# Key/value compression on TensorE: two tiles with strided rows, or four tiles with rows laid out by tap

## The reference, cut to what matters

```python
def compress(rows, pos_emb, w1, w2):
    B, T = rows.shape[0], rows.shape[1]
    r = rows.reshape(B, T // CMP_STRIDE, CMP_STRIDE, N_KV_HEADS, HEAD_DIM)   # CMP_STRIDE 16, HEAD_DIM 64
    w1h = w1.reshape(2, CMP_STRIDE, HEAD_DIM, HEAD_DIM)
    pe = pos_emb.reshape(2, CMP_STRIDE, 1, HEAD_DIM)
    lead = jnp.einsum('bnlgd,lde->bnge', r + pe[0], w1h[0])
    tail = jnp.einsum('bnlgd,lde->bnge', r + pe[1], w1h[1])
    return jnp.einsum('bnge,ef->bngf', jax.nn.silu(lead[:, :-1] + tail[:, 1:]), w2)
```

## Time and profile before

| | |
|---|---|
| timed runs | 1972.81, 1976.18, 1979.04 us |
| span of the profiled execution, first to last instruction | 1970.8 us |
| median of the timed runs less that span | 5.4 us |
| TensorE busy | 1854.6 us, 94% |
| VectorE, ScalarE, GpSimd busy | 888.9, 680.5, 173.2 us |
| mean DMA rate | 196 GB/s |

### The profile page before, as it was taken

The page is one execution under the profiler, slowest core; times in us unless marked ns, Lnnn a source line. Parts: engine busy times, 40 slices in busy tenths (PEclk is TensorE's granted clock), DMA queues, the critical chain, the costliest instruction groups (busy, mean ns, idle before and its releaser), DMA issues.

```text
span 1970.8 us, 34994 instructions
## 1 busy us (share of the span) xinstructions
PE 1854.6 (94%) x13870; PEld 1679.5 (85%) x13870; DVE 888.9 (45%) x1329; ACT 680.5 (35%) x813; POOL 173.2 (9%) x306
## 2 busy tenths in 40 slices
PE   4797589999999999999998999999999999999996
PEld 1297585885799999889996899999999999999995
DVE  1232132462644554545556544444444444444555
ACT  1122021562643443433334433333333333333333
POOL 1023000210322232101000100000000000000000
PEclk9689799999999999999999899999999999999998
DMA  9968864562844454487646544444455444443441
GB/s 363 407 240 242 213 232 173 210 263 104 318 162 161 160 162 151 169 303 308 242 171 241 198 159 169 170 155 140 160 169 194 164 170 156 163 170 132 162 164 58
DMA packets 67113, 386.81 MB, mean 196 GB/s; under 512 B 13661, under 2 KB 14077, under 8 KB 30062
## 3 DMA queue, kind: packets, MB, share of 16 engines
q1 hardware_dynamic: 50832, 346.39, 47.7%
q0 software_dynamic: 13904, 36.40, 6.9%
q10 hardware_dynamic: 2318, 3.19, 0.4%
HBM read 372.73 MB, written 13.20 MB: 196 GB/s over the span
## 4 chain that ended last, share of the span: by engine, by line
PE 82%; DMA 10%; DVE 3%; ACT 2%; ACTq 1%; issue 1%; SPq 0%; DVEq 0%
PE bank L635 24%; PE bank L637 23%; PE bank L636 23%; DMA raw<-in_w_units 10%; PE bank L738 3%; PE bank L646 3%; DVE wlo L345 1%; ACTq L973 1%; ACT whi L338 1%; PE bank L920 1%; PE bank L808 1%; PE bank L868 1%; PE bank L655 1%; PE bank L880 0%; PE bank L814 0%
## 5 line engine op out<-in xcount | busy, mean ns | idle before, releaser
L635 PE MATMUL bank<-xhi,wlo 128*128 128x288 f32 x2768 | 833.2, 301 | 38.2 <-DVE wlo L345 35.8
L636 PE MATMUL bank<-xlo,whi 128*128 128x288 f32 x2768 | 822.9, 297 | 0.0
L637 PE MATMUL bank<-xhi,whi 128*128 128x288 f32 x2768 | 819.7, 296 | 0.0
L345 DVE TENSOR_TENSOR wlo<-raw,whi 128x2048 fp32r<-128x2048 f32 (+1 forms) x251 | 532.8, 2123 | 544.1 <-ACT whi L338 536.5
L338 ACT CAST whi<-raw 128x2048 fp32r<-128x2048 f32 (+1 forms) x251 | 443.7, 1768 | 528.2 <-PE bank L637 390.2
L635 PEld LDWEIGHTS bank<-xhi,wlo 128*128 128x128 f32 x2768 | 525.1, 190 | 57.9 <-issue 42.0
L637 PEld LDWEIGHTS bank<-xhi,whi 128*128 128x128 f32 x2768 | 527.3, 191 | 0.0
L636 PEld LDWEIGHTS bank<-xlo,whi 128*128 128x128 f32 x2768 | 526.2, 190 | 0.4
L637 PE MATMUL bank<-hhi,whi 128*128 128x288 f32 x704 | 208.7, 296 | 0.0
L635 PE MATMUL bank<-hhi,wlo 128*128 128x288 f32 x704 | 208.0, 296 | 0.0
L636 PE MATMUL bank<-hlo,whi 128*128 128x288 f32 x704 | 205.2, 292 | 0.0
(11 more groups left out here) (275 smaller groups left out, 1460.9 us busy)
## 6 DMA issues: line engine op xcount, KB each, us to landing
raw<-in_w_units SPq DMA_DIRECT2D x284, 1024.0 KB, 5.4
raw<-in_w_ffn_out_units SPq DMA_DIRECT2D x64, 704.0 KB, 4.1
mgate<-mg POOLq DMA_DIRECT2D x32, 144.0 KB, 2.1
mgl<-mgate POOLq DMA_DIRECT2D x16, 288.0 KB, 5.3
toep<-rrow POOLq DMA_DIRECT2D x4, 1024.0 KB, 47.5
bz<-toep POOLq DMA_DIRECT2D x16, 192.0 KB, 2.7
xt<-in_x ACTq DMA_DIRECT2D x1, 2304.0 KB, 12.6
z<-in_x POOLq DMA_DIRECT2D x1, 2304.0 KB, 9.3
```

What stands on the lines that cost most here:

```text
L345: nc.vector.tensor_tensor(wlo[e][:, 0:size], raw[:, s, 0:size], f32(whi[e][:, 0:size]), ALU.subtract).then_inc(raw_used[s], 1)
L635: pe.matmul(acc, wlo[e][:, w], mh[:, c0 + kk, :], start=start and kk == 0, stop=False)
L636: pe.matmul(acc, whi[e][:, w], ml[:, c0 + kk, :], start=False, stop=False)
L637: m = pe.matmul(acc, whi[e][:, w], mh[:, c0 + kk, :], start=False, stop=stop and kk == kin - 1)
```

## The change

The cache pages and the embedding row come from the host laid out by tap: within each 128 positions, first tap 0 of the 8 chunks, then tap 1, and so on. GpSimd's copy of the prompt's rows makes the same order, in two copies. So one tap's columns are runs of 8 adjacent floats, one run per 128 positions. The lead and tail taps no longer accumulate in one place: for each of 16 taps there are four matmuls over all 16 chunks (19 x 16 = 304 columns), lead into the same half of bank 5, tail into the other half of bank 2, so that the four use the four quarters of the array. ScalarE copies the tail's halves from bank 2 to SBUF, swapping them back; VectorE adds lead (chunks 0 to 14) and tail (chunks 1 to 15) into `hsum`; ScalarE's Silu reads `hsum`, with the embedding row's sum as bias. TensorE waits in addition for bank 2 to be free. `wad` keeps only the two 64 x 64 blocks instead of a zero-padded 128 x 128, and GpSimd copies them in two steps. VectorE's last recurrent iteration is written out behind its loop to hold the second add.

```diff
-            one(pool.memset(cmp_rows[:, 2 * NSEQ, CMP:PAST], 0.0), rows_cp, 1)
+            one(pool.memset(cmp_rows[:, 2 * NSEQ, PAGE:PAST], 0.0), rows_cp, 1)
...
-                one(pool.tensor_copy(seqs[:, :, DEC_B, :], kvT[:, 0, 2 * kv:2 * kv + 2, 0:TP]), rows_cp, 2 + kv)
+                for g in range(2):
+                    one(pool.tensor_copy(seqs[:, g, DEC_B, :].rearrange("p (k l n) -> p k l n", k=2, l=STRIDE),
+                                         kvT[:, 0, 2 * kv + g, 0:TP].rearrange("p (k n l) -> p k l n", k=2, l=STRIDE)),
+                        rows_cp, 2 * kv + g + 2)
...
-                    one(pool.tensor_copy(wcur[:], wad[:, :, bass.ds(c, 1), :].squeeze(2)), wc_ok, c + 1)
+                    for h in range(2):
+                        half = slice(64 * h, 64 * h + 64)
+                        one(pool.tensor_copy(wcur[half, :, half], wad[half, :, bass.ds(c, 1), :].squeeze(2)),
+                            wc_ok, c * 2 + (h + 1))
...
-                pe.wait_ge(rows_cp, 2 + kv)
+                pe.wait_ge(rows_cp, 2 * kv + 3)
                 pe.wait_ge(gt_ok, 1)
                 after(pe, kc_ok, 2 * kv)
-                for l in range(CMP):
-                    for h in range(2):
-                        half = slice(64 * h, 64 * h + 64)
-                        ins = pe.matmul(bank[5][half, 0:(2 * NSEQ + 1) * NCMP], w1d[half, l, :],
-                                        cmp_rows[half, :, l:l + STRIDE * (NCMP - 1) + 1:STRIDE], start=l == 0, stop=l == CMP - 1)
+                pe.wait_ge(vt_ok, 1)
+                after(pe, rg_act, (RNN.n - 1) * 2 * kv)
+                rows = cmp_rows[:].rearrange("p r (k l n) -> p (r k) l n", k=2, l=STRIDE)
+                for l in range(STRIDE):
+                    for tap in range(2):
+                        for h in range(2):
+                            half = slice(64 * h, 64 * h + 64)
+                            to = half if tap == 0 else slice(64 - 64 * h, 128 - 64 * h)
+                            ins = pe.matmul(bank[5 if tap == 0 else 2][to, 0:CROWS * CHUNKS], w1d[half, l + STRIDE * tap, :],
+                                            rows[half, :, l, :], start=l == 0, stop=l == STRIDE - 1)
                 ins.then_inc(cmp_mm, 1)
...
                 act.wait_ge(cmp_mm, kv + 1)
+                after(act, cmp_sum, kv)
                 n = 2 * NSEQ * NCMP
-                nc.scalar.copy(cbias[:], bank[5][:, n:n + 1]).then_inc(cb_ok, 1)
-                act.wait_ge(cb_ok, kv + 1)
+                for h in range(2):
+                    nc.scalar.copy(tail[64 * h:64 * h + 64, :], bank[2][64 - 64 * h:128 - 64 * h, 0:CROWS * CHUNKS]).then_inc(tail_cp, 1)
+                act.wait_ge(cmp_sum, kv + 1)
                 dst = hk[:] if kv == 0 else hv[:].rearrange("p g s n -> p (g s n)")
-                nc.scalar.activation(dst, bank[5][:, 0:n], ACT.Silu, bias=cbias[:]).then_inc(cmp_act, 1)
+                nc.scalar.activation(dst, hsum[:, 0:n], ACT.Silu, bias=hsum[:, n:n + 1]).then_inc(cmp_act, 1)
...
+            def compress_sum(kv):
+
+                dve.wait_ge(tail_cp, 2 * kv + 2)
+                after(dve, cmp_act, kv)
+                lead = bank[5][:, 0:CROWS * CHUNKS].rearrange("p (r n) -> p r n", n=CHUNKS)
+                late = tail[:].rearrange("p (r n) -> p r n", n=CHUNKS)
+                v.tensor_tensor(hsum[:].rearrange("p (r n) -> p r n", n=NCMP), lead[:, :, 0:NCMP], late[:, :, 1:CHUNKS],
+                                ALU.add).then_inc(cmp_sum, 1)
...
                     split_lo(dve, RNN, i, j + 1)
+                    if kv is not None and j == 1:
+                        compress_sum(kv)
...
-            recurrent(0, False)
-            with dve.Fori(1, RNN.n) as i:
+            recurrent(0, False, 0)
+            with dve.Fori(1, RNN.n - 1) as i:
                 ch.loop(i - 1, 16)
                 recurrent(i)
-            ch.end(RNN.n - 1)
+            ch.end(RNN.n - 2)
+            recurrent(RNN.n - 1, True, 1)
             chain_rnn(2 * RNN.n - 1)
```

More of the change, by code:

```diff
@@ L38 @@
 NSEQ = 1 + DEC_B
+CROWS = 2 * NSEQ + 1
 H, KVH, HD = 16, 4, 64
@@ L42 @@
 STRIDE, CMP = 16, 32
-NCMP = PAST // STRIDE - 1
+CHUNKS = PAST // STRIDE
+NCMP = CHUNKS - 1
 DR = 1024
@@ L218, in build @@
         rrow = sbuf(p1, "rrow", [H, RV])
-        cmp_rows = sbuf(p1, "cmp_rows", [P, 2 * NSEQ + 1, PAST])
+        cmp_rows = sbuf(p1, "cmp_rows", [P, CROWS, PAST])
         rxp = sbuf(p1, "rxp", [P, LPAD])
@@ L227, in build @@
         hk = sbuf(p1, "hk", [P, 2 * NSEQ * NCMP])
+        tail = sbuf(p1, "tail", [P, CROWS * CHUNKS])
+        hsum = sbuf(p1, "hsum", [P, CROWS * NCMP])
         w1d = sbuf(p1, "w1d", [P, CMP, HD])
@@ L234, in build @@
         rb = sbuf(p1, "rb", [P, 2, RC])
-        wad = sbuf(p1, "wad", [P, 2, RC, P])
+        wad = sbuf(p1, "wad", [P, 2, RC, HD])
         convw = sbuf(p1, "convw", [P, 4, RC])
@@ L242, in build @@
         wcur = sbuf(p1, "wcur", [P, 2, P])
-        cbias = sbuf(p1, "cbias", [P, 1])
         p1.close()
@@ L309, in build @@
         rows_in, rows_cp, w1_in, cmp_mm, cmp_act = sem("rows_in"), sem("rows_cp"), [sem("w1k_in"), sem("w1v_in")], sem("cmp_mm"), sem("cmp_act")
+        tail_cp, cmp_sum = sem("tail_cp"), sem("cmp_sum")
         w2_mm, kc_ok = sem("w2_mm"), sem("kc_ok")
@@ L325, in build @@
         stored, y_out = sem("stored"), sem("y_out")
-        dve_c, pool_c, act_c, cb_ok = sem("dve_c"), sem("pool_c"), sem("act_c"), sem("cb_ok")
+        dve_c, pool_c, act_c = sem("dve_c"), sem("pool_c"), sem("act_c")
         def f32(ap):
@@ L437, in _ @@
             for n, (dst, v) in enumerate(((condp, 0.0), (f32(whi[0][:]), 0.0), (f32(wlo[0][:]), 0.0), (selt, 0.0), (rel1[32:33, :], 1.0),
-                           (w2b, 0.0), (wad, 0.0), (ones, 1.0 / D), (epst, EPS), (gs, 0.0))):
+                           (w2b, 0.0), (wcur, 0.0), (ones, 1.0 / D), (epst, EPS), (gs, 0.0))):
                 one(pool.memset(dst if isinstance(dst, bass.AP) else dst[:], v), pool_set, n + 1)
@@ L447, in _ @@
                 for w, name in enumerate(("lru_wa", "lru_wi")):
-                    pool.dma_start(wad[half, w, :, half],
+                    pool.dma_start(wad[half, w],
                                    a[name].rearrange("(c a) d e -> a d c e", a=2)[h]).then_inc(w_in_s, 16)
             one(pool.memset(rxp[:, 0:3], 0.0), st_pre, 1)
-            one(pool.memset(cmp_rows[:, 2 * NSEQ, CMP:PAST], 0.0), rows_cp, 1)
+            one(pool.memset(cmp_rows[:, 2 * NSEQ, PAGE:PAST], 0.0), rows_cp, 1)
             seqs = cmp_rows[:, 0:2 * NSEQ].rearrange("p (g s) t -> p g s t", s=NSEQ)
@@ L462, in load_rest @@
             def load_rest(kv):
-                pool.dma_start(cmp_rows[:, 2 * NSEQ, 0:CMP], a["cmp_pos"][kv]).then_inc(rows_in, 16)
+                pool.dma_start(cmp_rows[:, 2 * NSEQ, 0:PAGE], a["cmp_pos"][kv]).then_inc(rows_in, 16)
                 kv_written(pool)
-                one(pool.tensor_copy(seqs[:, :, DEC_B, :], kvT[:, 0, 2 * kv:2 * kv + 2, 0:TP]), rows_cp, 2 + kv)
+                for g in range(2):
+                    one(pool.tensor_copy(seqs[:, g, DEC_B, :].rearrange("p (k l n) -> p k l n", k=2, l=STRIDE),
+                                         kvT[:, 0, 2 * kv + g, 0:TP].rearrange("p (k n l) -> p k l n", k=2, l=STRIDE)),
+                        rows_cp, 2 * kv + g + 2)
             pool.wait_ge(b_in, SMALL)
@@ L763, in recurrent @@
                         pe.wait_ge(conv_ok, c + 1)
-                        pe.wait_ge(wc_ok, c + 1)
+                        pe.wait_ge(wc_ok, c * 2 + 2)
                         after(pe, rg_act, c)
@@ L1342, in chain_rnn, with recurrent @@
                                 gy[:, TP:T].rearrange("p (b s) -> p b s", s=DEC_S), ALU.mult).then_inc(y_ok, 1)
-            def recurrent(i, before=True):
+            def compress_sum(kv):
[5 more added lines that the diff above has]
+                                ALU.add).then_inc(cmp_sum, 1)
+            def recurrent(i, before=True, kv=None):
                 for j in range(4):
@@ L1649, in keys, with taps @@
         return np.ascontiguousarray(k_.reshape(n, t, 2, 2, HD).transpose(0, 3, 4, 2, 1).reshape(n, P, 2, t))
+    def taps(k_):
+        n, _, two, t = k_.shape
+        return k_.reshape(n, P, two, t // STRIDE, STRIDE).swapaxes(3, 4).reshape(n, P, two, t)
     slc, cmp_, win = cache_slc_kv[0], cache_cmp_kv[0], cache_win_kv[0]
@@ L1675, in lay_out @@
         selq[32 * q + np.arange(NSEQ), np.arange(NSEQ)] = 1.0
-    pos = cmp_pos[0].transpose(0, 2, 1)
+    pos = np.zeros((2, HD, STRIDE, PAGE // STRIDE), np.float32)
+    pos[:, :, :, 0:2] = cmp_pos[0].reshape(2, 2, STRIDE, HD).transpose(0, 3, 2, 1)
+    pos = pos.reshape(2, HD, PAGE)
     w1 = cmp_w1[0].transpose(0, 2, 1, 3)
@@ L1690, in lay_out @@
         "lru_wa": lru_wa[0], "lru_wi": lru_wi[0],
-        "cmp_k": keys(cmp_[:, :, 0]), "cmp_v": keys(cmp_[:, :, 1]), "slc_k": keys(slc[:, :, 0]),
```

(1 more changed line is left out.)

## The result

The changed kernel took 1932.8 us (median of four runs, 1929.76 to 1933.52); the kernel before, on the same chip, 1974.54 us (four runs, 1972.81 to 1979.04). The ratio is 0.9773, 95% interval 0.9755 to 0.9791: faster by 2.3%. The two medians themselves are 41.7 us apart. The forecast was 1931.

What follows compares the result with a forecast made beforehand. TensorE was taken to bound the kernel, with two 30.78 us stretches on its path. Span 1970.8 minus 44.9 saved by the matmuls gave 1925.9, plus 5.4 around the span 1931 us; all other parts 0; range 1926 to 1949.

Steps and rivals of the forecast that it cites:

- What bounds the kernel: Whole kernel: TensorE, busy 94% of the span; the changed step is two stretches of 30.78 us on its path.
- The matmuls: Changed step at L738: 32 sets of four tiles at 0.26 us, 8.3 us instead of 30.78, saving 44.9 us over both stretches.
- loads in fours each 0.26 us: Sign of a right forecast: the changed matmuls' weight loads come in fours every 0.26 us, with a stretch of 8.3 us.
- R1: Changed matmuls: tiles on different rows take double time however they read; stretch 16.6 us, total 1947.9 us; chance 0.13.
- R2: Changed matmuls: runs of eight floats pay a part for jumps; set 0.39, stretch 12.5, total 1939.6 us; chance 0.08.
- R3: Changed matmuls: four tiles run in turn, slower; sets 1.04 to 2.05 us, total 1981 to 2046 us; chance 0.05.
- The way out of the bank: ScalarE's tail copies and VectorE's add after the matmuls: about 1.3 us more, within 5.13 us of idle, nothing on the path.
- Under 4: Sign of a right forecast: ScalarE's idle before the next copy shrinks from 5.1 to under 4 us.
- VectorE's, TensorE's and GpSimd's new waits: VectorE's add, TensorE's wait for bank 2, GpSimd's split copies: all hidden, 0 us.
- the 99.6 us: GpSimd: a wait that the prediction put behind the memset cut from 2048 columns to 256, so costing 0.
- What is late next: Between the stretches: weight and page loads still arrive in time, 103.0 us kept within 1 us; a collision costs at most 4.3.
- The sum: Whole kernel: span 1970.8 - 44.9 = 1925.9 us, plus 5.4 between span and median, 1931 us; chance 0.74.

Runs made afterwards that it cites:

- the square of four kernels: Kernel after with two or four tiles, rows as before or by tap: stretches 32.79 (neither), 16.87 (four tiles alone), 16.52 (layout alone), 8.35 us (both).
- four_runs1: Kernel after with four tiles but rows in the order of before (runs of one float, step of 16): 16.87 us a stretch, median 1949.44 us.
- the two-tile kernel: Kernel after with rows by tap but two tiles, the tail in the same half as the lead: 16.52 us a stretch, median 1947.31 us.

## Why the prediction was right

*What bounds the kernel.* Right: two stretches on TensorE's path, shortened by 44.9 us in sum, and nothing behind them moved by more than 0.3 us.

*The matmuls.* Right. The set of four was put at 0.26 us from L646's 0.84 ns a column; it measured 8.35 / 32 = 0.261. The cause that was chosen for today's double price, the 16-float step, is shown by the square of four kernels. Of the two facts that no row separated, the tiles on different rows are innocent. The argument used for that in the prediction, loads starting in pairs, was weaker than it looked: it holds at the strided price, where the loads of four_runs1 come in fours, but at the full rate the view shows one unbroken row, so the sign that was announced ("loads in fours each 0.26 us") could not be seen in it. The length of the stretch decided.

*R1.* Fell by the two-tile kernel. What it leaned on, that tiles on different rows can't use one bank at the same time, does not bind here, where their outputs are on different partitions of it: 0.258 us a pair in bank 5.

*R2.* Fell: runs of eight cost what runs of four cost, 8.35 us, 0.86 ns a column. Runs of two do pay a part, but 9.33 us a stretch and not R2's 12.5, 2 us of span.

*R3.* Fell. Sets of four cost 0.261, far under 0.962.

*The way out of the bank.* Costed at 1.3 us more, 0.8 for the copies and 0.5 for the add; the idle shrank by 0.74, because ScalarE's table load does not wait for VectorE's add, and because the copy to `cbias` that goes (0.16 us at 348.46 before) was not taken off. Covered either way. "Under 4" was wrong by this: 4.39.

*VectorE's, TensorE's and GpSimd's new waits.* Right, all hidden. The add began at 328.86, near the expected 326.7 and the 2.0 us of later start. One wait was misread, with nothing resting on it: the 99.6 us lie ahead of GpSimd's memset; behind it lie the 99.09 before the copy of the prompt's rows.

*What is late next.* Right: 103.27 against 103.00 us, though the tap weights and pages fell on the tail of the refill.

*The sum.* Right in size, with one term misread. The 5.4 us between span and median were taken as what lies around the span. The profiled run of the kernel after took 1929.76 us with a span of 1928.2: 1.6 us lie around it. If as much lies around the span of before, its profiled run took 1972.4 us, and the other 3.8 are only its place among the runs. The later start of the first stretch is such scatter too: the same kernel run again has it at 315.72 us, and with the loop written out, identical up to there, at 320.75. That the forecast lies within 2 us of the measured 1932.8 is therefore in part luck: the same kernel took 1927.37 us in the later session. The differences of the medians, 41.7 us here and 46.5 there, lie on both sides of the 44.9 that the stretches give.

The chain of the kernel after run again, then of the kernel with the loop written out:

```profile
315.72 8.35 PE bank L753 x128
```

```profile
320.75 8.35 PE bank L753 x128
```

## What to carry to other kernels

Where an f32 moving operand is read with a step, look at how many of its columns share 16 bytes: with one, every column here cost 1.69 to 1.75 ns instead of 0.85 to 0.86, and laying the data out so that four do, on the host or in a copy that is hidden anyway, halved the matmul time. Matmuls of 64 rows and 64 outputs halve it once more if a sum is split over the unused quarters of the array and added afterwards on an idle engine; count the free microseconds of that engine first. A matmul made shorter pays only where TensorE itself is what the stage waits for: the same form at the gates shortened the matmuls by 0.5 us a set, and the kernel did not get faster.

## What the runs showed of the hardware that was not expected

A step of four floats costs as much as a step of 16 (17.03 and 16.87 us a stretch), while a step of two is almost free (8.67 to 8.78). Two columns in 16 bytes are not quite four: runs of two cost 12% (9.33 us), a step of two 4 to 5%, and the runs do not say why these two differ. Four f32 tiles, all four quarters of the array, two row halves writing into each of two banks, took 0.261 us for 304 columns, 0.86 ns a column; L646's four tiles of 32 columns took 0.84 and L920's full array 0.91. And TensorE's clock can fall, or not, behind nearly the same idle (0.75 and 1.91 us, 0.47 and 2.08): in three traces of the same instructions there (the kernel after twice, and with the loop written out) it fell to 0.77 in one.
